# Two-layer hybrid encoder step: weight splits, low parts and first heads placed elsewhere in the three norm passages

## What is computed

```python
for i in range(2):
    for grp in range(2):                          # prompt, sample
        sh1, sc1, gt1, sh2, sc2, gt2 = adaln(cs[grp], w_ada[i], b_ada[i])
        h = modulate(rms_norm(x, norm_mix[i]), sh1, sc1)
        mix = gla_mixer(h, ...) if i == 0 else diff_attention(h, ...)
        x = x + gt1[:, None, :] * mix
        h = modulate(rms_norm(x, norm_ffn[i]), sh2, sc2)
        f, cst_new = conv_ffn(h, cst, ffn_w_in[i], ffn_conv_w[i], ffn_conv_b[i], ffn_w_out[i])
        xs[grp] = x + gt2[:, None, :] * f
```

## Time and profile before

| | before |
|---|---|
| time, median of 3 executions | 1394.04 us (1393.62 to 1394.4) |
| the profiled execution, its own time | 1394.21 us |
| its span, first to last instruction | 1392.3 us |
| TensorE busy | 1367.9 us |
| VectorE busy | 948.0 us |
| ScalarE busy | 656.0 us |
| GpSimd busy | 89.2 us |
| weights and the like moved | 182.41 MB, mean 131 GB/s |
| granted TensorE clock, mean | 1.00 |

### The profile page before, as it was taken

How to read it: one execution, slowest core, us unless ns; L and a number is a source line. 1 busy time by engine, 2 the same in 40 slices (tenths; PEclk the granted TensorE clock), 3 DMA queues, 4 the chain that set the end, 5 groups by cost and what they waited for, 6 DMA issues and landing times.

```text
span 1392.3 us, 26066 instructions
## 1 busy us (share of the span) xinstructions
PE 1367.9 (98%) x10754; PEld 1301.4 (93%) x10754; DVE 948.0 (68%) x1591; ACT 656.0 (47%) x1462; POOL 89.2 (6%) x149
## 2 busy tenths in 40 slices
PE   9999999999999999999999999999899999999999
PEld 6889889999999999999888888889899999999999
DVE  5678677579889788778765646576798653554554
ACT  5543444466553353251565655653665542552430
POOL 0000000200000000000300000000200000000000
PEclk9999999999999999999999999999999999999999
DMA  9644542244435444534423323112343222223222
GB/s 378 239 153 162 178 152 84 98 153 153 151 132 186 167 145 147 179 129 150 168 108 106 116 90 134 63 61 93 106 152 136 82 71 92 91 69 114 76 71 103
DMA packets 38013, 182.41 MB, mean 131 GB/s; under 512 B 4294, under 2 KB 6854, under 8 KB 26632
## 3 DMA queue, kind: packets, MB, share of 16 engines
q1 hardware_dynamic: 22984, 126.98, 26.0%
q0 software_dynamic: 14912, 53.78, 11.2%
HBM read 172.82 MB, written 7.91 MB: 130 GB/s over the span
## 4 chain that ended last, share of the span: by engine, by line
PE 89%; DVE 5%; ACT 3%; issue 2%; DMA 1%; POOL 0%; SPq 0%; DVEq 0%; POOLq 0%; ACTq 0%
PE ps L656 26%; PE ps L658 26%; PE ps L657 25%; PE ps L1054 2%; PE ps L1104 1%; DVE sq L1722 1%; DVE h_lo L1735 1%; PE ps L1013 1%; PE ps L1076 1%; ACT w_hi L1162 1%; PE ps L694 1%; PE ps L746 1%; PE ps L894 0%; DVE xT L1811 0%; DMA xT<-in_xT 0%
## 5 line engine op out<-in xcount | busy, mean ns | idle before, releaser
L658 PE MATMUL ps<-h_hi,w_lo 128*128 128x272 f32 x2048 | 592.2, 289 | 0.0
L656 PE MATMUL ps<-h_hi,w_hi 128*128 128x272 f32 x1952 | 569.5, 292 | 5.7 <-ACT up L1442 1.7
L657 PE MATMUL ps<-h_lo,w_hi 128*128 128x272 f32 x1952 | 561.4, 288 | 0.0
L658 PEld LDWEIGHTS ps<-h_hi,w_lo 128*128 128x128 f32 x2048 | 384.9, 188 | 0.0
L656 PEld LDWEIGHTS ps<-h_hi,w_hi 128*128 128x128 f32 x1952 | 367.4, 188 | 14.8 <-issue 4.9
L657 PEld LDWEIGHTS ps<-h_lo,w_hi 128*128 128x128 f32 x1952 | 367.8, 188 | 1.1 <-issue 1.0
L1162 ACT CAST w_hi<-w_raw 128x2048 fp32r<-128x2048 f32 (+2 forms) x106 | 179.2, 1691 | 193.7 <-PE ps L658 169.2
L1650 DVE TENSOR_TENSOR w_lo<-w_raw,w_hi 128x2048 fp32r<-128x2048 f32 (+2 forms) x105 | 215.1, 2049 | 63.5 <-ACT w_hi L1162 63.0
L657 PE MATMUL ps<-act_lo,w_hi 128*128 128x272 f32 (+1 forms) x704 | 203.8, 290 | 0.0
L656 PE MATMUL ps<-act_hi,w_hi 128*128 128x272 f32 (+1 forms) x704 | 203.5, 289 | 0.0
L658 PE MATMUL ps<-act_hi,w_lo 128*128 128x272 f32 (+1 forms) x704 | 203.2, 289 | 0.0
(11 more groups left out here) (289 smaller groups left out, 1769.9 us busy)
## 6 DMA issues: line engine op xcount, KB each, us to landing
w_raw<-in_wst SPq DMA_DIRECT2D x72, 1024.0 KB, 4.9
a_raw<-in_ada_r POOLq DMA_DIRECT2D x56, 512.5 KB, 4.7
w_raw<-in_wst SPq DMA_DIRECT2D x28, 768.0 KB, 4.3
a_raw<-in_ada_g POOLq DMA_DIRECT2D x24, 512.0 KB, 3.6
a_pro<-in_ada_p SPq DMA_DIRECT2D x8, 1024.0 KB, 16.5
v_raw<-in_wst SPq DMA_DIRECT2D x8, 1024.0 KB, 9.1
w_raw<-in_wst SPq DMA_DIRECT2D x10, 512.0 KB, 4.5
xT<-in_xT SPq DMA_DIRECT2D x4, 544.0 KB, 5.2
```

What stands on the lines that cost most here:

```text
L656: mm(out, lhs_hi, rhs_hi, start=first, stop=False)
L657: mm(out, lhs_hi, rhs_lo, start=False, stop=False)
L658: return mm(out, lhs_lo, rhs_hi, start=False, stop=last)
```

## The change

Five things are done.

1. **First heads.** ScalarE copies u0 and u1 of an MLP's first block ahead of silu. VectorE clears the edge columns (`clear_edges`) ahead of the last two tiles of the second half, and no longer at the start of `ffn`.
2. **Low parts.** In passage 2 VectorE makes `w_lo` of dk(0) in four pieces: one behind each of the first three output units, the last behind `make_gain`. In passage 3 it makes `w_lo` of up(1,0,0) in two: one where it stood, one behind the output of B10.
3. **Second block's high passes.** In passage 3 TensorE runs, for each tile of the first half, the two matmuls with `w_hi` of u2 and of u3 besides the six of u0 and u1; the matmuls with `w_lo` of u2 and u3 follow behind the loop. Ahead of the loop it waits for `w_hi` of the second block and for the banks of u2 and u3.
4. **Split moved.** For that, ScalarE splits up(1,0,1) at the start of the passage: one half ahead of the first square, the other behind the second.
5. **Banks.** u6 and u7 of the dk/dq pair take the banks of u2 and u3 (2 and 3) in place of those of u0 and u1 (0 and 1).

```diff
@@ -133,7 +133,7 @@
         kind = BL[n][0]
         if BL[n] in PAIRED:
             at = u - FIRST_U[BN[next(a for a, z in PAIRS if BL[n] in (a, z))]]
-            b = at % 4 if kind in ("gout", "down") else PAIR_BANKS[at]
+            b = at % 4 if kind in ("gout", "down") or kind in ("dk", "dq") and at >= 6 else PAIR_BANKS[at]
         elif kind == "up" and BL[n][2:] == (0, 2):
             b = (4, 5, 7, 6)[u - FIRST_U[n]]
         elif BL[n] in KMAJOR:
@@ -777,15 +777,32 @@
                         pe.wait_ge(w_lo_ok, BN[name] + 1)
                     for u in us[4 * half:4 * half + 2]:
                         bank_free(u)
+                    ahead = which == 3 and half == 0
+                    if ahead:
+                        pe.wait_ge(w_hi_ok, BN[name] + 2)
+                        for u in us[2:4]:
+                            bank_free(u)
                     for k in range(KT):
                         pe.wait_ge(h_ok, H_BASE[stage] + KT * half + k + 1)
                         for u in us[4 * half:4 * half + 2]:
                             ins = three(*unit_terms(u, k), k == 0, k == KT - 1)
                             if k == KT - 1:
                                 ins.then_inc(unit_done, 1)
+                        if ahead:
+                            for u in us[2:4]:
+                                out, w_h, _, x_h, x_l = unit_terms(u, k)
+                                mm(out, w_h, x_h, start=k == 0, stop=False)
+                                mm(out, w_h, x_l, start=False, stop=False)
                         if half == 0 and k == 6:
                             stats(which, 1)
-                    if half == 0:
+                    if ahead:
+                        pe.wait_ge(w_lo_ok, BN[name] + 2)
+                        for u in us[2:4]:
+                            for k in range(KT):
+                                out, _, w_l, x_h, _ = unit_terms(u, k)
+                                ins = mm(out, w_l, x_h, start=False, stop=k == KT - 1)
+                            ins.then_inc(unit_done, 1)
+                    elif half == 0:
                         units(us[2:4])
                     elif which == 2:
                         unit(us[6])
@@ -1447,6 +1464,9 @@
                 ub = 0
                 act.wait_ge(conv_in, 16)
                 act.wait_ge(crow_in, 48 + 16 * l)
+                first = BN[("up", l, 0, 0)]
+                head_in(BU[first][0], 0, l, tile)
+                head_in(BU[first][2], 1, l, tile)
                 A_(c_row[:, :, 0:D], c_row[:, :, 0:D], ACT.Silu).then_inc(crow_ok, 1)
                 for kind, c in FFN_ORDER:
                     if kind == "down":
@@ -1467,7 +1487,7 @@
                             x = up[:, t, :]
                             if BL[n] not in PAIR_OF:
                                 head_in(u0, t, l, tile)
-                            elif t == 0:
+                            elif t == 0 and n != first:
                                 head_in(u0, 0, l, tile)
                                 head_in(BU[n][2], 1, l, tile)
                             act.wait_ge(unit_done, u1 + 1)
@@ -1611,7 +1631,11 @@
             heads_turned(NPAIR - 1, 1, 5)
             heads_turned(NPAIR - 1, 2, 6)
             split(BN[("up", 1, 0, 0)])
-            for m in range(KT):
+            split(BN[("up", 1, 0, 1)], 0)
+            square(3, 0, 0)
+            square(3, 1, 0)
+            split(BN[("up", 1, 0, 1)], 1)
+            for m in range(2, KT):
                 square(3, m, 0)
             for m in range(3):
                 square(3, m, 1)
@@ -1625,10 +1649,7 @@
             square(3, 6, 1)
             square(3, 7, 1)
             half_modulated(3, 0, (3,))
-            split(BN[("up", 1, 0, 1)], 0)
-            half_modulated(3, 0, (4, 5))
-            split(BN[("up", 1, 0, 1)], 1)
-            half_modulated(3, 0, range(6, KT))
+            half_modulated(3, 0, range(4, KT))
             half_root(3, 1)
             half_modulated(3, 1, range(KT))
             ffn(1)
@@ -1639,16 +1660,16 @@
             step = Steps(dve, dve_step)
             TT, STT = dve.tensor_tensor, dve.scalar_tensor_tensor
 
-            def low(n, part=None):
+            def low(n, part=None, parts=2):
                 if n >= NB:
                     return
                 m = block_kt(n) * BC
                 dve.wait_ge(w_hi_ok, n + 1)
                 if n:
                     dve.wait_ge(w_lo_ok, n)
-                c0, c1 = (0, m) if part is None else (part * m // 2, (part + 1) * m // 2)
+                c0, c1 = (0, m) if part is None else (part * m // parts, (part + 1) * m // parts)
                 ins = TT(low_cols(w_lo, n, c0, c1), low_cols(w_raw, n, c0, c1), f32(hi_cols(n, c0, c1)), ALU.subtract)
-                if part != 0:
+                if part in (None, parts - 1):
                     ins.then_inc(w_lo_ok, 1)
 
             def ada_add(i):
@@ -1736,6 +1757,10 @@
                                   op0=ALU.add, op1=ALU.subtract)
                     ins.then_inc(h_ok, 1)
 
+            def clear_edges():
+                for t in range(2):
+                    dve.memset(up[:, t, 0:2], 0.0).then_inc(conv_ok, 1)
+
             def stage_end(which, name, gate_row, junk_cols, before, n_ada):
                 def out(u):
                     n, t, half = UNITS[u]
@@ -1744,15 +1769,20 @@
 
                 n = BN[name + (2,)]
                 us = pair_units(name + (2,))
-                for u in us[0:2]:
-                    out(u)
                 if which == 1:
+                    for u in us[0:2]:
+                        out(u)
                     low(n + 2)
-                for u in us[2:4]:
-                    out(u)
+                    for u in us[2:4]:
+                        out(u)
+                else:
+                    for i, u in enumerate(us[0:4]):
+                        out(u)
+                        if i < 3:
+                            low(n + 2, i, 4)
                 make_gain(which, (0, KT), n_ada)
                 if which == 2:
-                    low(n + 2)
+                    low(n + 2, 3, 4)
                 out(us[4])
                 if which == 1:
                     half_tiles(which, 0, (0, 1))
@@ -1771,7 +1801,11 @@
                     out(us[7])
                     half_tiles(which, 0, range(4, KT))
                     low(n + 3)
-                half_tiles(which, 1, range(KT))
+                half_tiles(which, 1, range(KT - 2))
+                if which == 1:
+                    dve.wait_ge(conv_in, 16)
+                    clear_edges()
+                half_tiles(which, 1, range(KT - 2, KT))
 
             def output_lo(src, stage, k):
                 dve.wait_ge(h_hi_ok, H_BASE[stage] + k + 1)
@@ -2024,9 +2058,6 @@
                     for _ in range(k):
                         ada_rows((FFN_ROWS_DONE, ROWS_DONE)[l])
 
-                dve.wait_ge(conv_in, 16)
-                for t in range(2):
-                    dve.memset(up[:, t, 0:2], 0.0).then_inc(conv_ok, 1)
                 for kind, c in FFN_ORDER:
                     if kind == "down":
                         if c == 0:
@@ -2211,7 +2242,7 @@
             heads_low(NPAIR - 1, 1, 5)
             heads_low(NPAIR - 1, 2, 6)
             evacuate(DOUT_A[-TAIL_A + 2])
-            low(BN[("up", 1, 0, 0)])
+            low(BN[("up", 1, 0, 0)], 0)
             evacuate(DOUT_A[-TAIL_A + 3], False)
             def last_out(us):
                 for u in us:
@@ -2220,14 +2251,18 @@
 
             last_out(DOUT_B[0:KT])
             make_gain(3, (0, KT), 44)
-            last_out(DOUT_B[KT:KT + 4])
+            last_out(DOUT_B[KT:KT + 3])
+            low(BN[("up", 1, 0, 0)], 1)
+            last_out(DOUT_B[KT + 3:KT + 4])
             half_tiles(3, 0, (0,))
             last_out(DOUT_B[KT + 4:KT + 6])
             half_tiles(3, 0, (1,))
             last_out(DOUT_B[KT + 6:])
             half_tiles(3, 0, range(2, KT))
             low(BN[("up", 1, 0, 1)])
-            half_tiles(3, 1, range(KT))
+            half_tiles(3, 1, range(KT - 2))
+            clear_edges()
+            half_tiles(3, 1, range(KT - 2, KT))
             ffn(1)
```

## The result

The changed kernel takes **1405.25 us** in the median (four runs, 1403.69 to 1406.54), the kernel before 1393.83 in the same session: a ratio of 1.0074, 95% interval 1.0055 to 1.0094, so 8 to 13 us slower. TensorE's busy time hardly moved; the time is in its waits.

What follows compares the result with a forecast made beforehand. TensorE, busy 1367.9 of 1392.3 us, was taken as the bound, so only its waits could change. Terms -0.1 + 1.3 + 7.1 + 1.2 = +9.5 on 1394.2 gave 1403.7 us, range 1400.8 to 1406.2.

Steps and rivals of the forecast that it cites:

- First heads, passage 1: Passage 1: copies ahead of silu remove TensorE's 0.78 wait, but up(0,0,2)'s low part is late next; -0.1 us (-0.4 to +0.1).
- Passage 2: Low part of dk(0) in pieces plus later banks for u6: +0.5 up to +1.7 us, taken as +1.3.
- the pieces: Passage 2: low-part pieces could start the tile loop 0.85 us sooner or, delaying GpSimd's adds, up to 0.35 later.
- Passage 3, the split: ScalarE's moved half cast waits for weights, squares queue behind; GpSimd's second add +3.8 us, TensorE's sums +4.6.
- low piece: Passage 3: second piece of up(1,0,0)'s low part runs beside GpSimd's adds; 0 to 1.15 us more, taken as 0.8.
- the landing: Passage 3: weights of up(1,0,1), issued at 969.28, land 5.3 us later, at 974.6; ScalarE stands still until then.
- Passage 3, the loop: Start set by outputs of B14 and B15, ten matmuls per tile; second-half sums +7.2 us, up(1,0,2) +7.1 (+6.2 to +7.5).
- The clock: Passage 3: TensorE's 5.7 us wait drops its clock to half; between 0 and 2.2 us, taken as +1.2.
- The clock holds: Rival: no clock fall in passage 3's wait, everything else as forecast; 1402.5 us, chance 0.25.
- The pieces cost nothing: Rival: GpSimd and VectorE share the gaps in passages 2 and 3; 1400.8 us, 1402.0 with the clock's fall; chance 0.12.
- The clock stays low longer: Rival: passage 3's tile loop too starts at half pace, some +3 us; 1406.7 us, chance 0.08.
- Not slower: Rival: up(1,0,1)'s weights land by about 968, squares run on time, passage 3 gives -2.3; 1393.1 us, chance 0.05.

Runs made afterwards that it cites:

- Run 10: Kernel before with only the two first head copies of each up-block group put ahead of silu; 1395.29 us against 1393.76.
- run 2: Changed kernel, new tile loop kept, but the split of up(1,0,1) put behind the eight first-half squares and first modulated tile; 1401.73 us against 1393.76 for the kernel before.
- run 3: Changed kernel with the split of up(1,0,1) in its old place and the ordinary tile loop; 1397.00 us against 1393.75 for the kernel before.
- run 7: Kernel before with only the low part of dk(0) in four pieces between the outputs of passage 2; 1394.62 us against 1393.75.
- run 1: Kernel before with only the split of up(1,0,1) moved, its halves ahead of the first square and behind the second; 1398.54 us against 1393.75.
- run 9: Changed kernel plus 18 identity multiplications ahead of passage 3's first sums and 8 ahead of its tile loop; 1403.37 us against 1393.94 for the kernel before.
- run 5: Kernel before with only banks 2 and 3 for u6 and u7 of the dk/dq pair; 1396.40 us against 1393.75.
- run 6: Kernel before with the u6 and u7 bank change plus eight identity multiplications ahead of u6 of passage 2; 1395.14 us against 1393.81.
- run 4: Kernel before with only the low part of up(1,0,0) halved, its second half behind the output of B10; 1394.61 us against 1393.76.

## Why the prediction came out as it did

Predicted 1403.7 (1400.8 to 1406.2), measured 1405.25: the sign, the places and most sizes were right, and what is missing is clock.

- **First heads, passage 1** (-0.1, between -0.4 and +0.1): -0.27, with the wait for `w_lo` in place of the wait for `up`, as forecast. Run 10 adds what the text had not seen: the copies wait for the edge memsets, and without their move this part would cost 0.66.
- **Passage 2** (+1.3 for pieces and banks): +1.57. The banks are 1.37 to 1.39 (1.33 forecast), the pieces +0.53 alone, just over the +0.35 that I took for their upper end. In runs 2 and 3, with the same passage, the stretch is +2.04 and +2.13. The mis-sized step is how much of the sums' delay reaches the tile loop. From up(0,0,2) on, the first-half sums are 0.93, 1.22, 1.39 and 1.48 later than before (changed kernel, runs 7, 2 and 3), the second-half sums 0.24, 0.53, 0.70 and 0.80: all but some 0.69 passes on, where my sum let 1.6 shrink to 0.35. Why the sums' own delay differs between executions of the same passage was not tried.
- **Passage 3, the split** (squares +3.8, low piece +0.8, sums +4.6): the squares' delay is there, and the wait for the sums 4.71 (5.7 forecast; my own terms, 0.40 + 4.6 + 0.5, give 5.5). From the last attention output to the sums it is +3.94. The step that was too large is the landing: the load took 4.6 and not 5.3. The low piece was sized rightly: the five adds take 5.16 beside it and 4.37 in run 1, where it is missing, and from the last attention output the sums come 3.94 and 3.40 later than before; the load landed 0.3 sooner in the changed kernel, which is why the two differ by less than 0.79.
- **Passage 3, the loop** (start set by VectorE's outputs, second-half sums +7.2, up(1,0,2) +7.1): the releasers are those forecast, and without a fall in this passage the stretch is +6.69 (run 9). Alone the parts are 3.34 (run 1, at the sums) and 4.9 (run 2), more than the whole: part of the late sums lies under the loop's own wait.
- **The clock** (+1.2, between 0 and 2.2): this is the term that failed. Its upper bound was read from the pace of the first 18 matmuls, where the trace prints a granted clock of 1.00 (0 to 8 us), so that row does not show what a fall costs. One fall costs 1.47 to 1.50 where TensorE has work all along (behind u6 in runs 2, 5 and 9), and 1.49 in passage 3 (the changed kernel against run 9), so its size was near. What I had left out is the number of falls: I looked at the wait of 5.7 alone, while the wait of 2.0 that the banks put ahead of u6 goes with a mean clock below 1.000 in seven of eleven executions (run 5), and with that wait filled nine of eleven stay at 1.000 (run 6). Without clock the sum is 1394.2 - 0.27 + 1.57 + 6.69 = 1402.2, close to the 1402.60 of run 9's execution at full clock; the median is 3.0 above, as much as two falls. That there were two is argued and not shown: the profiled execution, the fastest, had one; the two slowest of the four have a mean clock of 0.996 where it has 0.998, but the one of 1405.1 has 0.998 too. If all that is missing is the clock's, the term came to 3.0, above its upper bound of 2.2. The sum without it is nearer (1402.2, forecast 1402.5) than its parts are: passages 1 and 3 came to 0.6 less than forecast, passage 2 to 0.3 more.

**The rivals.** "The clock holds" falls, though its 1402.5 is what the kernel would take. "The pieces cost nothing" falls with run 7. "The clock stays low longer" has the right total for the slowest runs (1406.54 against 1406.7); its place, a loop at half pace, is not in this trace, though run 2's has it (0.50 from 990 to 992). "Not slower" needed a landing by 968; the cast ran at 975.21.

**Open.** Where the clock fell in the executions that were not traced, and why the same passage brings a fall in one execution and none in the next (a wait of 2.02 us with none in run 3, waits up to 1.37 us with one in run 5). The low piece was never taken out of the changed kernel alone; its 0.8 is the difference between two kernels that also differ in the loop.

## What to carry over

Before a step is put early of an in-order engine's queue, look up when its last input lands and what stands behind it: a cast of 1 us that waits for a load cost 3.3 us, since the squares of a critical sum queued behind it. A loop that does more for each tile also wants more banks before its first one, and what frees the last of them decides its start. And a new wait of 2 us on TensorE is not priced by its length alone, as the pace behind it may be halved for several microseconds; a few idle multiplications in it show how much of a loss is that. What an engine is given in a gap can also cost on another engine: look at who works beside it on the same memory (run 4).
